# First layer of a two-block transformer kernel: gate product between the compression products, compressed softmax in two halves, twelve gate chunks ahead of the attention, output weights split over sixteen steps

## The reference, cut to what matters

```python
def nsa_mixer(u, ...):            # u = rmsnorm(x); 512 tokens, 16 heads of 64, 4 key groups
    q, k_cmp, v_cmp, k_sel, v_sel, k_win, v_win, gate, z = split(u @ w_in)
    k_cmp, v_cmp = mlp(blocks of 32 keys), mlp(blocks of 32 values)   # 31 blocks
    s_c = q @ k_cmp + bias_c
    p_c = softmax(where(m_c, s_c, NEG)) * any(m_c)
    o_c = p_c @ v_cmp
    ...                           # o_s: selected keys, o_w: window keys, each a softmax attention
    o = gate[..., 0:1] * o_c + gate[..., 1:2] * o_s + gate[..., 2:3] * o_w
    o = o.reshape(b, s, NSA_WIDTH) * silu(z)
    return o @ w_out
```

## Time and profile before

| | us |
|---|---|
| median of 3 runs | 1403.68 (1401.01 to 1405.08) |
| the profiled execution | 1405.38 |
| its span, first to last instruction | 1403.6 |
| PE busy in the span | 1346.3 (96%) |
| POOL / ACT / DVE busy | 764.0 / 747.4 / 658.6 |

### The profile page before, as it was taken

How to read it: one execution, slowest core, us unless ns; L and a number is a source line. 1 busy time by engine, 2 the same in 40 slices (tenths; PEclk the granted TensorE clock), 3 DMA queues, 4 the chain that set the end, 5 groups by cost and what they waited for, 6 DMA issues and landing times.

```text
span 1403.6 us, 20936 instructions
## 1 busy us (share of the span) xinstructions
PE 1346.3 (96%) x7738; PEld 1101.8 (79%) x7738; DVE 658.6 (47%) x1609; ACT 747.4 (53%) x1572; POOL 764.0 (54%) x786
## 2 busy tenths in 40 slices
PE   6999999998999999999999999999999999999997
PEld 5878778886888787878788888778889887778885
DVE  4352566766251444554330011881463347887135
ACT  4252388888343465665442333892534355887252
POOL 4452257665753555665553525687546534586652
PEclk9999999999899999999999999999999999999999
DMA  6242011111424322221343232424226322002322
GB/s 245 94 151 91 15 32 61 40 37 61 165 80 133 133 75 77 89 79 58 150 180 120 92 110 98 144 98 167 104 73 222 113 88 64 1 16 101 140 91 60
DMA packets 28901, 138.66 MB, mean 99 GB/s; under 512 B 3584, under 2 KB 4096, under 8 KB 18048
## 3 DMA queue, kind: packets, MB, share of 16 engines
q1 hardware_dynamic: 15200, 98.05, 19.9%
q10 hardware_dynamic: 13600, 39.27, 8.1%
HBM read 127.86 MB, written 8.39 MB: 97 GB/s over the span
## 4 chain that ended last, share of the span: by engine, by line
PE 79%; DVE 7%; ACT 6%; POOL 4%; issue 2%; DMA 2%; SPq 0%; POOLq 0%; ACTq 0%; DVEq 0%
PE psum L523 47%; PE psum L557 10%; PE psum L1459 4%; PE psum L1487 3%; PE psum L1416 3%; PE psum L1507 2%; DVE w_free L1568 2%; PE psum L1070 2%; POOL w_lo L478 2%; PE psum L1044 2%; PE psum L766 1%; PE psum L1472 1%; POOL w_free L1699 1%; ACT w_free L956 1%; ACT x_r L1628 1%
## 5 line engine op out<-in xcount | busy, mean ns | idle before, releaser
L478 POOL TENSOR_TENSOR w_lo<-w_raw,w_hi 128x512 fp32r<-128x512 f32 (+3 forms) x153 | 392.4, 2580 | 277.5 <-ACT w_hi L467 268.2
L467 ACT ACTIVATE w_hi<-w_raw 128x2048 fp32r<-128x2048 f32 (+1 forms) x89 | 158.5, 1781 | 91.2 <-DMA w_raw<-in_weights 77.2
L523 PE MATMUL psum<-w_hi,split 128*128 128x512 f32 x608 | 197.7, 399 | 4.0 <-POOL w_lo L478 4.0
L523 PE MATMUL psum<-u_lo,w_hi 128*128 128x512 f32 (+1 forms) x428 | 169.9, 397 | 2.1 <-POOL w_lo L478 2.1
L523 PE MATMUL psum<-u_hi,w_hi 128*128 128x512 f32 (+1 forms) x428 | 167.8, 392 | 0.0
L523 PE MATMUL psum<-u_hi,w_lo 128*128 128x512 f32 (+1 forms) x428 | 167.7, 392 | 0.0
L956 ACT ACTIVATE w_free<-w_free,neg_max 128x512 f32<-128x512 f32 (+3 forms) x256 | 148.3, 584 | 11.4 <-DVE neg_max L1568 10.3
L523 PEld LDWEIGHTS psum<-w_hi,split 128*128 128x128 f32 x608 | 116.0, 191 | 29.0 <-POOL w_lo L478 5.0
L523 PE MATMUL psum<-w_hi,u_lo 128*128 128x512 f32 (+2 forms) x352 | 134.4, 382 | 2.1 <-DVE u_lo L916 1.8
L523 PE MATMUL psum<-w_lo,u_hi 128*128 128x512 f32 (+2 forms) x352 | 132.6, 377 | 0.0
L523 PE MATMUL psum<-w_hi,u_hi 128*128 128x512 f32 (+2 forms) x352 | 132.6, 377 | 0.0
(11 more groups left out here) (237 smaller groups left out, 2787.4 us busy)
## 6 DMA issues: line engine op xcount, KB each, us to landing
w_raw<-in_weights SPq DMA_DIRECT2D x83, 1024.0 KB, 4.8
x<-x_scratch ACTq DMA_DIRECT2D x12, 512.0 KB, 4.9
w_raw<-in_weights SPq DMA_DIRECT2D x10, 512.0 KB, 4.0
gain<-in_gains ACTq DMA_DIRECT2D x9, 512.0 KB, 5.0
gain<-in_strips ACTq DMA_DIRECT2D x16, 256.0 KB, 2.8
spare<-in_strips ACTq DMA_DIRECT2D x16, 256.0 KB, 2.9
x_scratch<-x ACTq DMA_DIRECT2D x8, 512.0 KB, 4.0
gain<-in_near ACTq DMA_DIRECT2D x8, 512.0 KB, 4.3
```

The lines of the kernel that those rows point to most:

```text
L467: high = nc.scalar.activation(w_hi[b][:, c], w_raw[b][:, c], ACT.Copy)
L478: low = nc.gpsimd.tensor_tensor(w_lo[b][:, c], w_raw[b][:, c], w_hi[b][:, c].bitcast(F32), ALU.subtract)
L523: mm = nc.tensor.matmul(dst, lhs, rhs, start=(a == 0 and k == 0 and (wl, ul) == (0, 1)), stop=(a + 1 == u and k + 1 == nk and (wl, ul) == ...
```

## The change: what it does

1. The branch gate runs between the two compression products, and the order of the weight units follows it.
2. The low part of the second compression unit is computed by DVE (`compress_weights_low`) instead of POOL.
3. The compressed scores of the last two groups lie inside the first four quarter products of `nsa_k`, a quarter in each.
4. The compressed softmax runs in two halves, each over two groups.
5. The output gate: twelve chunks ahead of the attention (eight, then the transposes of the compressed map, then four), four in each of rounds 0 and 2, two in each round after, so that the last chunk lies in round 46. The first tile is taken by ACT before the attention loop. The tiles rotate over four places instead of three, one of them in `gain[1]`, so `load_gain(1)` moves behind the attention.
6. Both output units are split inside the loop: ACT at steps 51 to 58 (quarters), POOL at steps 53 to 68 (eighths).

```diff
 _run("nsa_cmp0", 1, (16,), 128, "compress")
+_run("nsa_gate", 1, (8,), GATES, "features")
 _run("nsa_cmp1", 1, (16,), 128, "compress")
-_run("nsa_gate", 1, (8,), GATES, "features")
...
+        def compress_weights_low(dve):
+
+            n = RUNS["nsa_cmp1"]["unit"]
+            b = SLOT[n]
+            dve.wait_ge(w_high, n + 1)
+            nc.vector.tensor_tensor(w_lo[b][:], w_raw[b][:], w_hi[b][:].bitcast(F32), ALU.subtract).then_inc(cmp1_low, 1)
...
-        Z_FIRST = 6
         Z_BANK = 7
+        Z_FIRST, Z_EARLY = KC + KC // 2, KC // 2
 
         def z_step(t):
 
-            return max(0, KC * (t + 1) - Z_FIRST - 1) // 2 * 2 + 1
+            return 1 if t == 1 else KC * t - 9
+
+        def z_round(d):
+
+            return (Z_FIRST + Z_EARLY * d, Z_EARLY) if d < 2 else (Z_FIRST + 2 * Z_EARLY + 2 * (d - 2), 2)
...
             if f is nsa_flow:
-                z_fill(pe, 0, Z_FIRST)
+                z_fill(pe, 0, KC)
                 for g in range(3):
                     compress_turn_tensor(pe, g)
+                z_fill(pe, KC, Z_FIRST - KC)
...
                 if f is nsa_flow:
-                    z_fill(pe, Z_FIRST + i, 2)
+                    z_fill(pe, *z_round(i // 2))
...
-                    for t in range(KC):
+                    for t in range(1, KC):
                         if i == z_step(t) + 2:
                             z_take(act, t)
-                        if t >= 2 and i == z_step(t - 2) + 3:
+                    for t in range(2, KC):
+                        if i == (z_step(t - 2) + 3 if t > 2 else 1):
                             z_high_part(act, t)
-                    if f.steps - 4 <= i < f.steps:
-                        split_high(act, NSA_OUT, i - f.steps + 4, 4)
+                    if 51 <= i < 59:
+                        split_high(act, NSA_OUT + (i - 51) // 4, (i - 51) % 4, 4)
...
+                if f is nsa_flow and i == 2:
+                    z_low_part(pool, 2, 0)
+                    z_low_part(pool, 2, 1)
...
-                    for t in range(2, KC):
-                        if i - z_step(t - 2) - 5 in (0, 1):
-                            z_low_part(pool, t, i - z_step(t - 2) - 5)
-                    if f.steps - 3 <= i <= f.steps:
-                        split_low(pool, NSA_OUT, i - f.steps + 3)
-                    if i == f.steps + LAG + 2:
-                        split_low(pool, NSA_OUT + 1)
+                    for t in range(3, KC):
+                        if i - z_step(t - 2) - 4 in (0, 1):
+                            z_low_part(pool, t, i - z_step(t - 2) - 4)
+                    if 53 <= i < 69:
+                        split_low(pool, NSA_OUT + (i - 53) // 8, (i - 53) % 8, 8)
...
             compress_hidden_tensor(pe, 0)
+            project_tensor(pe, "nsa_gate", banks=1, base=6)
             compress_hidden_tensor(pe, 1)
-            project_tensor(pe, "nsa_gate", banks=1, base=6)
...
             project_tensor(pe, "nsa_q1", between=beside_q1)
-            for j in range(NT):
-                compress_scores_tensor(pe, 1, j)
-            project_tensor(pe, "nsa_k")
+            project_tensor(pe, "nsa_k", between={(0, 0, j): beside_first_k(pe, j) for j in range(NT)})
...
-            compress_softmax_vector(dve)
+            compress_softmax_vector(dve, 0)
+            compress_softmax_vector(dve, 1)
```

More of the change, by code:

```diff
@@ L469, in split_high, with split_low @@
                 high.then_inc(w_high, 1)
-        def split_low(pool, n, part=None, parts=4):
+        def split_low(pool, n, part=None, parts=4, count=1):
             b = SLOT[n]
@@ L479, in split_low @@
             if part in (None, parts - 1):
-                low.then_inc(w_ready, 1)
+                low.then_inc(w_ready, count)
         def next_unit(run, i, a):
@@ L1410, in z_fill @@
                     if t == 0:
[L1411 removed]
+                        pe.wait_ge(cmp_shifted, 3)
                     else:
@@ L1668, in pair_scalar @@
                     high(i - LAG)
-                if i == (f.steps if f is na_flow else f.steps + LAG - 1):
+                if i == (f.steps if f is na_flow else f.steps + LAG - 1) and f is not nsa_flow:
                     split_high(act, RUNS[f.name + "_out"]["unit"] + 1)
@@ L1919, in compress_hidden_tensor @@
             b = SLOT[run["unit"]]
-            pe.wait_ge(w_ready, run["unit"] + 1)
+            pe.wait_ge(*((cmp1_low, 1) if a else (w_ready, run["unit"] + 1)))
             for o in range(16):
@@ L2044, in beside_last_q, with beside_first_k, compress_softmax_vector @@
             return lambda: compress_scores_tensor(pe, 0, j)
-        def compress_softmax_vector(dve):
+        def beside_first_k(pe, j):
+            return lambda: compress_scores_tensor(pe, 1, j)
+        def compress_softmax_vector(dve, gp):
             def spread(off):
-                return at(off, 64).unsqueeze(2).to_broadcast([P, 64, 32])
-            pc = at(N_PC, HEADS * NT * 32).rearrange("p (h c) -> p h c", c=32)
-            for g in range(4):
+                return at(off, 32).unsqueeze(2).to_broadcast([P, 32, 32])
+            pc = at(N_PC + gp * 2 * T, 2 * T).rearrange("p (h c) -> p h c", c=32)
+            largest, r = N_MX + 32 * gp, N_MX + 64 + 32 * gp
+            for g in (2 * gp, 2 * gp + 1):
                 dve.wait_ge(cmp_s, g + 1)
@@ L2057, in compress_softmax_vector @@
             settle("dve", dve)
-            done("dve", nc.vector.tensor_reduce(at(N_MX, 64), pc, AX, ALU.max))
+            done("dve", nc.vector.tensor_reduce(at(largest, 32), pc, AX, ALU.max))
             settle("dve", dve)
[L2060 to L2063, removed]
+            nc.vector.tensor_tensor(pc, pc, spread(largest), ALU.subtract).then_inc(cmp_shifted, 1)
+            dve.wait_ge(cmp_exp, gp + 1)
+            done("dve", nc.vector.tensor_reduce(at(r, 32), pc, AX, ALU.add))
             settle("dve", dve)
-            done("dve", nc.vector.reciprocal(r, r))
+            done("dve", nc.vector.reciprocal(at(r, 32), at(r, 32)))
             settle("dve", dve)
-            g0 = gate[:].rearrange("p (t g j b) -> p g t j b", t=NT, g=4, j=4)[:, :, :, :, 0]
-            by_tile = r.rearrange("p (g t j) -> p g t j", g=4, t=NT)
-            dve.wait_ge(bank_free["act"], 4 + RUNS["nsa_gate"]["taken"] + 4)
+            g0 = gate[:].rearrange("p (t g j b) -> p g t j b", t=NT, g=4, j=4)[:, 2 * gp:2 * gp + 2, :, :, 0]
+            by_tile = at(r, 32).rearrange("p (g t j) -> p g t j", g=2, t=NT)
+            dve.wait_ge(bank_free["act"], 4 + RUNS["nsa_cmp1"]["taken"] + 4)
             done("dve", nc.vector.tensor_tensor(by_tile, by_tile, g0, ALU.mult))
@@ L2073, in compress_softmax_vector @@
             settle("dve", dve)
-            nc.vector.tensor_tensor(pc, pc, spread(N_MX + 64), ALU.mult).then_inc(cmp_shifted, 1)
+            nc.vector.tensor_tensor(pc, pc, spread(r), ALU.mult).then_inc(cmp_shifted, 1)
         def compress_turned_bank(g):
@@ L2515, in _ @@
             first_scalar(act)
-            load_gain(act, 1)
             load_compress(act)
@@ L2546, in _ @@
             act.wait_ge(nsa_flow.gated, 2 * KC)
+            load_gain(act, 1)
             chain_scalar(act, diff_chain, "nsa_out", A["x"])
@@ L2615, in _ @@
             first_pool(pool)
-            for name in ("nsa_v", "nsa_kc", "nsa_q0", "nsa_cmp0", "nsa_cmp1", "nsa_gate", "nsa_q1"):
+            for name in ("nsa_v", "nsa_kc", "nsa_q0"):
+                project_pool(pool, name)
+            split_low(pool, RUNS["nsa_q1"]["unit"], count=2)
+            for name in ("nsa_cmp1", "nsa_q1"):
                 project_pool(pool, name)
```

27 lines of the change are left out of this document (16 added, 11 removed).

## The result

The changed kernel takes 1407.37 us (median of 14 runs, 1404.90 to 1409.95) against 1402.66 us for the kernel before beside it (14 runs): ratio 1.0034, 95% interval [1.0025, 1.0043]. It is slower by 4.7 us, where 8.8 us faster was predicted. Its profiled execution took 1407.09 us, with a span of 1405.3. That is only 1.7 above the profiled execution of before, which had more stretches at the lower clock later on (3.4 us each at 468 and 683, where after's has none; at half speed they cost half their length, 3.4 us together).

The account below looks back on a forecast made before the run. The prediction took PE, busy 96% of the span, to bound the kernel. Its terms, -3.8 + 6.0 - 8.8 - 2.2 = -8.8 us, took 1403.7 to 1394.9 us, with a range of 1391 to 1399, reaching on to 1402.

Parts of the forecast that it names:

- Middle: Attention steps 8 to 56: PE-bound, nothing altered but which chunk lies where; 0 us.
- step 3: Start of the attention, to the scores of step 6: 19.7 us become 25.7, with ten more chunks done; +6.0 us.
- 1, the gate between the products: Ahead of `nsa_q1`: the chain doesn't get shorter and the idle 1.8 us only splits in two; 0 us.
- 2, `nsa_k`: Compressed scores inside `nsa_k`, softmax in halves: 32.2 us become 28.4; -3.8 us.
- The rival in which the clock falls there: In `nsa_k` the clock falls all the same, which costs the 3.8 us back: 1398.7 us; chance 12%.
- 4, end: From the scores of step 48 to `first_output`: 52.4 us become 43.6, by POOL's count; -8.8 us.
- S: The start of the scores of attention step 48; `first_output` was forecast at S + 43.6.
- 5, behind it: Behind the start of `first_output`: the lower clock from 354.6 to 359.2 goes; -2.2 us.
- The end gives it back: End of the attention: ACT's and POOL's extra splits cost the upper bound, 49.5, and the lower clock stays: 1403 us; 15%.
- The slower rival: Last 16 attention steps: without gate chunks PE idles in every round and the clock falls: 1409 us; chance 7%.

Follow-up runs that it names:

- e2: The kernel before with eight gate chunks ahead of the attention instead of six and tile 0 taken ahead of the loop; 1414.66 us, ratio 1.0089.
- e1: The changed kernel with two output gate chunks instead of four in round 2, so fourteen ahead instead of sixteen; 1395.75 us, ratio 0.9957.
- e4: The changed kernel with a plain copy in place of the output gate's silu, so without its table loads; 1389.92 us, ratio 0.9913.
- e6: The changed kernel with the split of the gate tiles' weights two steps later on ACT and POOL, silu unmoved; 1405.04 us, ratio 1.0011.
- e9: e1 with the two output units split two steps later on ACT and POOL; 1393.03 us, ratio 0.9937 to the kernel before.
- e5: The changed kernel with twelve gate chunks ahead instead of sixteen, two in every round; 1414.95 us, ratio 1.0078 to the kernel before.

## Why the prediction was wrong, by its own steps

**Middle, the step that failed.** The prediction says of the middle (188.4 to 324.9 in before, from step 8 to 56) that it "is PE-bound and the change alters nothing in it but which chunk lies where". PE's busy 133.9 of 136.5 was read as a property of the stretch; it was a property of where ACT's 4.2 us of gate work stood in the pattern of eight steps. The same rows 6 that gave the table load and the silu in step 3 were not laid beside the steps at which they would come in the middle. It cost 9.8 us of the 13.5 by which the forecast missed (-8.8 to +4.7). e2 shows the cause alone in the old kernel and e1 shows it gone in the new. e4 and e6 show that table loads and tile split both take part. Why a place costs what it does is argued from the counts of ACT's steps, which find the best and the worst place and miss the sizes.

**1, the gate between the products: right.** The idle 1.8 is split in two as said, 0.5 ahead of `cmp1` and 1.4 ahead of `nsa_q1`. The chain of DMA, ACT and POOL starts 0.5 us earlier (88.51 for 89.07), so `nsa_q1` does too, at 99.99. The copies of the compressed values end at 106.0 (106.7 forecast), and PE does not wait for them.

**2, `nsa_k`: right.** From the end of `nsa_q1` to that of `nsa_k` pass 28.4 us, as forecast (130.50 to 158.92), at full clock, and no wait came from the softmax halves. The other 0.5 of the -4.3 are those of `nsa_q1`. The rival in which the clock falls there is out.

**3, start: right within its bounds.** 26.8 for 25.7 (23.5 to 28). PE is idle 3.0 us there, 2.7 were counted, in other pieces: 0.9 for the silu of tile 1 where 1.9 had been expected, and it resumes at 176.4 as forecast, but 1.2 for POOL's map ahead of it. ACT's step 1 waits for tile 2 as described, 1.66 us instead of 0.6, ahead of the table load that the exponentials need:

```profile
168.13 1.06 ACT L1438 ACTIVATE w_hi<-w_raw 128x1024 fp32r<-128x1024 f32 x1 [1.66 <-DMA w_raw<-in_weights]
169.21 1.28 ACT L964 ACT_TABLE_LOAD   x1
```

The fall of the clock that it allowed for came too (3.4 us at 177.6).

**4, end: POOL's pace right, its start 5 us late.** 46.9 for 43.6 (bounds 38.1 and 49.5). The count was S + 14.4 for POOL's first eighth, 25.8 from there until the map of step 61 is normalised, and 3.4 behind it. Measured are S + 19.7, 25.5 and 1.7. The eighths take 0.73 instead of 0.83, and POOL has one gap of 0.72 us from 345 to 362. The term that failed is "exponentials begin at S + 2 behind the last silu": they begin at 320.72, S + 5.9. The last silu is at step 49 with its two table loads, the same place as in the middle, and since round 46 there are no chunks left for PE to do meanwhile. So PE stands 2.83 us for the map of which ACT's part is late, and POOL waits for ACT's last quarter (PE's row, then POOL's, in after):

```profile
322.71 1.94 PE L1500 MATMUL psum<-ident,w_free 128*128 128x128 f32 x8 [2.83 <-DVE w_lo L1594]
334.53 0.73 POOL L479 TENSOR_TENSOR w_lo<-w_raw,w_hi 128x256 fp32r<-128x256 f32 x1 [1.62 <-ACT w_hi L468]
```

The output unit had landed long before: its DMA is issued at 314.94, and ACT's first quarter, at 325.18, follows the map before it without a gap. In this idle time of PE, from 319.88 to 322.71, the clock falls to its lower level:

```profile
320.90:327.70 6.80, 4.99 (x24) 5.02 (x25) 4.47 (x16) 5.59 (x18) 4.33 (x9) 0.50 0.12 48
```

With the silu and the splits two steps later the same stretch takes 44.8, at full clock (e9).

**5, behind it: right.** -2.1 for -2.2, with the clock at 1.00 from 361.9 on. `load_gain(1)` keeps nobody waiting: it is issued at 373.2, lands within 7 us, and DVE first reads the row at 382.3.

**The rivals.** "The end gives it back" (1403) did not hold: the end gave 5.5 us, where that rival had 2.9. The slower rival, the clock in rounds without chunks, had the right direction and the time nearest to the result (1409 for 1407.4), but by luck, since the cause is another: of the 28 us at half speed that it named, after has 6.8, behind the one long wait of 2.83 us, and in e9 those rounds run at 1.00. The case that came true, ACT's work out of its place, was not among them, and so the chance of 0.08 for slower and the upper end of 1402.0 were both too low.

**The sum on e9.** With the phase kept, the five stretches of e9 are -4.1, +4.9, -0.1, -7.6 and -2.1, together -9.1, where -3.8, +6.0, 0, -8.8 and -2.2 had been forecast. This bears out that the middle was the step that failed. It does not confirm the forecast of -8.8, since e9 is another kernel: it does two chunks fewer in its start and splits the output units later, and start and end miss by 1.1 and 1.2 in opposite directions.

## What to carry to other kernels

When work is moved by some steps in a software-pipelined loop, write down for each engine what it has to do in each step of the repeating pattern, and where the moved work lands in it; a busy share averaged over the pattern does not tell. An engine at 82 to 89% can still set the pace if several long instructions fall on its full steps. Move such work by a whole pattern, or to the steps with the least of that engine's own work, and don't put a wait for a transfer ahead of work that others need before its data can have landed (in e5 ACT stood 8.12 us for it). Look at the last piece of such work too: here it stood where PE had no gate chunks left, and cost 2.83 us of waiting at once.

## What was not expected of the hardware

A table load cost its 1.28 us and nothing else: the silu starts 0.02 us behind it (268.37 + 1.28, 269.67). But what two of them cost the kernel per eight steps went from about 0.5 us (on the condition named at e4) to 2.57 with their place.
